# Product 4 in a second Strassen step, in 18 of the 20 projection groups

## The reference

```
h = rmsnorm(x); proj = h @ w_in                     # 1024 x 14336
b, c, xv, z, q, k, v, z_b, g_a, g_b = split(proj)
y_a = (b * (conv3(c * xv) + bias) * silu(z)) @ w_a_out
q, k = rotary(q), rotary(k) / 16                    # 4 heads of 256
o    = chunkwise retention(q, k, v), decay per head # v: 4 heads of 512
y_b  = (rmsnorm(o) * silu(z_b)) @ w_b_out
out  = rmsnorm(x + (sigmoid(g_a) * y_a + sigmoid(g_b) * y_b) @ w_o)
```

## Time and profile before

| | |
|---|---|
| median of 3 runs | 1380.13 us |
| profiled execution | 1379.97 us, of which the span of the trace 1378.2 us |
| PE busy | 1366.2 us (99%) |
| DVE busy | 995.4 us (72%) |
| ACT, POOL busy | 575.3 us (42%), 392.4 us (28%) |
| one conv group / one turn group | 38.08 / 38.46 us |

### The profile page before, as it was taken

How to read it: one execution, slowest core, us unless ns; L and a number is a source line. 1 busy time by engine, 2 the same in 40 slices (tenths; PEclk the granted TensorE clock), 3 DMA queues, 4 the chain that set the end, 5 groups by cost and what they waited for, 6 DMA issues and landing times.

```text
span 1378.2 us, 16016 instructions
## 1 busy us (share of the span) xinstructions
PE 1366.2 (99%) x6174; PEld 1130.5 (82%) x6174; DVE 995.4 (72%) x952; ACT 575.3 (42%) x779; POOL 392.4 (28%) x276
## 2 busy tenths in 40 slices
PE   9999999999999999999999999999999999999997
PEld 8788888888888888888888888888888888888886
DVE  6898434356556555678988888647777898778897
ACT  7843233222222222233333333337787433433445
POOL 0100222233334444443344444315545000100012
PEclk9999999999999999999999999999999999999999
DMA  9646313322221222355443444547767689945443
GB/s 335 182 161 209 112 57 107 123 77 77 77 63 61 67 71 61 92 153 153 142 119 111 134 138 140 195 170 244 273 223 267 140 314 329 240 162 198 156 89 122
DMA packets 105035, 211.64 MB, mean 154 GB/s; under 512 B 6912, under 2 KB 48000, under 8 KB 100096
## 3 DMA queue, kind: packets, MB, share of 16 engines
q1 hardware_dynamic: 101936, 192.77, 41.9%
q0 software_dynamic: 2880, 17.83, 6.6%
q10 hardware_dynamic: 144, 0.02, 0.0%
HBM read 147.68 MB, written 54.53 MB: 147 GB/s over the span
## 4 chain that ended last, share of the span: by engine, by line
PE 90%; DVE 3%; ACT 2%; issue 2%; DMA 1%; POOL 1%; SPq 1%; POOLq 0%; ACTq 0%; DVEq 0%
PE psum L2282 19%; PE psum L2284 18%; PE psum L2285 18%; PE psum L2416 7%; PE psum L2417 7%; PE psum L2418 7%; PE psum L2250 2%; PE psum L2253 2%; PE psum L2252 2%; PE psum L2327 2%; PE psum L2329 2%; PE psum L2328 2%; DMA raw_b<-x_t 1%; PE psum L2368 1%; DMA value_scratch<-value_c 1%
## 5 line engine op out<-in xcount | busy, mean ns | idle before, releaser
L2282 PE MATMUL psum<-hc,slots 128*128 128x512 f32 x1120 | 436.3, 390 | 0.9
L2285 PE MATMUL psum<-hc,slots 128*128 128x512 f32 x1120 | 435.8, 389 | 0.0
L2284 PE MATMUL psum<-hc,slots 128*128 128x512 f32 x1120 | 435.8, 389 | 0.0
L1004 ACT ACTIVATE slots<-work 128x1024 fp32r<-128x1024 f32 x140 | 148.7, 1062 | 510.2 <-PE psum L2285 414.9
L2282 PEld LDWEIGHTS psum<-hc,slots 128*128 128x128 f32 x1120 | 210.2, 188 | 47.2 <-issue 3.6
L1479 DVE TENSOR_TENSOR slots<-work,slots 128x1024 fp32r<-128x1024 f32 x140 | 185.5, 1325 | 86.8 <-ACT slots L1004 86.8
L2285 PEld LDWEIGHTS psum<-hc,slots 128*128 128x128 f32 x1120 | 210.2, 188 | 43.6
L2284 PEld LDWEIGHTS psum<-hc,slots 128*128 128x128 f32 x1120 | 210.2, 188 | 43.4
L1254 ACT ACTIVATE last_slot<-arena 128x1024 fp32r<-128x1024 f32 x112 | 118.6, 1062 | 163.2 <-PE psum L2418 155.7
L2416 PE MATMUL psum<-last_slot 128*128 128x512 f32 (+1 forms) x452 | 175.3, 388 | 0.0
L2417 PE MATMUL psum<-last_slot 128*128 128x512 f32 (+1 forms) x452 | 175.0, 387 | 0.0
(11 more groups left out here) (188 smaller groups left out, 1826.7 us busy)
## 6 DMA issues: line engine op xcount, KB each, us to landing
work<-w_channel SPq DMA_DIRECT2D x80, 512.0 KB, 3.6
arena<-w_last SPq DMA_DIRECT2D x19, 1024.0 KB, 7.5
qk<-qk_scratch SPq DMA_DIRECT2D x32, 512.0 KB, 3.4
arena<-w_last POOLq DMA_DIRECT2D x9, 1024.0 KB, 10.5
v_raw<-value_scratch SPq DMA_DIRECT2D x32, 256.0 KB, 3.9
arena<-gate_scratch SPq DMA_DIRECT2D x16, 512.0 KB, 6.9
value_c<-w_value SPq DMA_DIRECT2D x10, 512.0 KB, 4.2
rows_of_x<-x_rows SPq DMA_DIRECT2D x8, 512.0 KB, 9.3
```

The costliest lines, as they stand in the source:

```text
L1004: nc.scalar.activation(slots[:, u % SLOTS, 0, :], src, ACT.Copy).then_inc(w_hi, 1)
L2282: nc.tensor.matmul(bank, slot[:, 0, w], x_high, start=product in STARTS and j == 0, stop=False, skip_group_check=True)
L2284: nc.tensor.matmul(bank, slot[:, 0, w], x_low, start=False, stop=False, skip_group_check=True)
L2285: last = nc.tensor.matmul(bank, slot[:, 1, w], x_high, start=False, stop=j == 3, skip_group_check=True)
```

## The change

In groups 1 to 18 (`TWICE`) product 4 is itself done by a Strassen step on quarters: its d quadrant of weights is cut in four (columns of `work`, in the new `TILE_ORDER`), and so is T4 of h, in two halves of depth and two halves of 256 tokens. Seven products of quarters replace eight; each is 2 tiles of depth by 3 matmuls of 256 columns, so 42 matmuls of 256 columns stand for 24 of 512. Product 4 becomes two units. The first has the products of the plain weights of quarters 11, 12 and 21; the second has four products of sums of weights. POOL makes those sums in place after the low part of the first unit (`second_sums`, four operations of 128x256), and only then are they split, as 768 columns.

Three products go straight into the banks of product 4. The others go to two banks that the next group's product 6 is to use (`second_bank`), and DVE adds them to the group's sum: `second_first` after the first unit, `second_rest` (three operations) after the second. PE's last quarter product accumulates in the bank that `second_first` reads, so it waits for it. The next group's product 6 waits for `second_rest`. The sums of h's quarters are made once, in group 0, by DVE and ACT; the third goes over a part of T4, whose old content is kept in HBM and loaded again for group 19. `s1(g+1)` now waits for the low part of the second unit. The area for software DMA descriptors is set to 4 KB to make room.

```diff
+TWICE = range(1, GROUPS - 1)
+UNIT_TABLE = [(g, p) for g in range(GROUPS) for p in range(8 if g in TWICE else 7)]
+TILE_ORDER = [(0, 0), (0, 1), (0, 2), (0, 3), (1, 2), (1, 3), (1, 0), (1, 1)]
...
         def s1(g):
-            pool.wait_ge(w_ready, unit_at(g - 1, 4) + 1 if g else unit_of(1, 3, 1) + 1)
+            pool.wait_ge(w_ready, ended_at(g - 1) + 1 if g else unit_of(1, 3, 1) + 1)
...
+        def second_sums(g):
+            d = work[ROLES[g]["d"]]
+            a11, a12, a22, a21 = (d[:, n * QUARTER:(n + 1) * QUARTER] for n in range(4))
+            pool.wait_ge(w_ready, unit_at(g, 4) + 1)
+            nc.gpsimd.tensor_tensor(a22, a21, a22, ALU.add).then_inc(summed, 1)
+            nc.gpsimd.tensor_tensor(a21, a11, a21, ALU.subtract).then_inc(summed, 1)
+            pool.wait_ge(summed, second_summed(g, 1))
+            nc.gpsimd.tensor_tensor(a11, a22, a11, ALU.subtract).then_inc(summed, 1)
+            pool.wait_ge(summed, second_summed(g, 3))
+            nc.gpsimd.tensor_tensor(a12, a12, a11, ALU.subtract).then_inc(summed, 1)
...
+            if g in TWICE:
+                second_sums(g)
             if g + 1 < GROUPS:
                 s1(g + 1)
...
+        def second_first(g):
+            dve.wait_ge(unit_done, unit_at(g, 4) + 1)
+            at = tp_v[g % 2][:, 0, 0:QUARTER]
+            nc.vector.tensor_tensor(at, psum[:, second_bank(g), 0:QUARTER], at, ALU.add).then_inc(value_sum, 1)
+        def second_rest(g):
+            dve.wait_ge(unit_done, ended_at(g) + 1)
...
+                nc.vector.tensor_tensor(at, product, at, ALU.add).then_inc(value_sum, 1)
...
             if VALUE_UNITS < u <= UNITS:
-                g, n = divmod(u - 1 - VALUE_UNITS, 7)
-                if ORDER[n] not in (1, 2):
+                g, n = place_of(u - 1)
+                if n == 6 and g in TWICE:
+                    second_first(g)
+                elif n == 7:
+                    second_rest(g)
+                    add(g, 4)
+                elif ORDER[n] not in (1, 2):
                     add(g, ORDER[n])
             if u + 2 < UNITS:
                 low(u + 2)
...
+        def second_units(g):
+            u, x, z = unit_at(g, 4), set_at(g, 4), second_bank(g)
...
+            product_of_quarters(u, 0, quarter(0), one_six, start=True)
+            product_of_quarters(u, 1, quarter(2), c11)
+            product_of_quarters(u, 2, second("T4"), c21).then_inc(unit_done, 1)
+            pe.wait_ge(w_ready, u + 2)
+            product_of_quarters(u + 1, 2, second("T1"), five, start=True)
+            product_of_quarters(u + 1, 3, second("T3"), seven, start=True)
+            product_of_quarters(u + 1, 1, quarter(3), c12)
+            pe.wait_ge(value_sum, second_added(g, 1))
+            product_of_quarters(u + 1, 0, second("T2"), one_six).then_inc(unit_done, 1)
...
         def unit(g, product):
+            if product == 6 and g - 1 in TWICE:
+                pe.wait_ge(value_sum, second_added(g - 1, 4))
...
-    nc = bacc.Bacc("TRN2", target_bir_lowering=False, num_devices=1)
+    nc = bacc.Bacc("TRN2", target_bir_lowering=False, num_devices=1, dynamic_dma_scratch_size=4 * KB)
```

More of the change, by code:

```diff
@@ L95, in unit_at, with ended_at, columns_of, place_of @@
 def unit_at(g, product):
-    return VALUE_UNITS + 7 * g + ORDER.index(product)
+    return VALUE_UNITS + UNIT_TABLE.index((g, ORDER.index(product)))
+def ended_at(g):
+    return unit_at(g, 4) + (g in TWICE)
+def columns_of(u):
+    return 3 * QUARTER if u >= VALUE_UNITS and place_of(u)[0] in TWICE and place_of(u)[1] == 6 else 2 * HALF
+def place_of(u):
+    return UNIT_TABLE[u - VALUE_UNITS] if u < UNITS else (GROUPS, u - UNITS)
+def summed_until(g):
+    return 16 + 4 * g + 4 * len([n for n in TWICE if n < g])
+def second_summed(g, n):
+    return summed_until(g) + 4 + n
+def second_added(g, n):
+    return 20 + 4 * (g - TWICE.start) + n
 def before(order, product):
@@ L585, in _ @@
         stores = {"gate": gate_stores, "conv": conv_stores, "turn": turn_stores}
+        sp.wait_ge(h_ready, made(4))
+        for part in range(2):
+            sp.dma_start(kept_d[:, part], t4_part(1, part).bitcast(F32)).then_inc(x_in[4], 16)
         for g in range(GROUPS):
@@ L1365, in _ @@
                 continue
-            g, p = divmod(u - VALUE_UNITS, 7)
+            g, p = place_of(u)
+            if g == 0 and p == 5:
+                for name in ("T1", "T2", "T4"):
+                    second_high(name)
+            if g == TWICE.start and p == 2:
+                second_high("T3")
             if 0 < g <= GROUPS:
@@ L2254, in value_unit, with product_of_quarters, quarter, second @@
             last.then_inc(unit_done, 1)
+        def second_units(g):
+            u, x, z = unit_at(g, 4), set_at(g, 4), second_bank(g)
+            c11, c12, c21 = (psum[:, x + n // 2, n % 2 * QUARTER:(n % 2 + 1) * QUARTER] for n in range(3))
+            one_six, five, seven = psum[:, z, 0:QUARTER], psum[:, z + 1, 0:QUARTER], psum[:, z + 1, QUARTER:HALF]
+            def product_of_quarters(unit, place, right, to, start=False):
+                slot = slots[:, unit % SLOTS]
+                for j in range(2):
+                    w = slice((2 * place + j) * P, (2 * place + j + 1) * P)
+                    high, low = (right(part)[:, j, :] for part in range(2))
+                    nc.tensor.matmul(to, slot[:, 0, w], high, start=start and j == 0, stop=False, skip_group_check=True)
+                    nc.tensor.matmul(to, slot[:, 0, w], low, start=False, stop=False, skip_group_check=True)
+                    last = nc.tensor.matmul(to, slot[:, 1, w], high, start=False, stop=j == 1, skip_group_check=True)
+                return last
+            def quarter(n):
+                return lambda part: t4_part(n, part)
+            def second(name):
+                return lambda part: second_part(name, part)
+            pe.wait_ge(w_ready, u + 1)
+            pe.wait_ge(sum_made, 5 * g + sums_until(ORDER, 7))
+            if g == TWICE.start:
+                pe.wait_ge(h_ready, made(3) + 4)
+            product_of_quarters(u, 0, quarter(0), one_six, start=True)
[7 more added lines that the diff above has]
+            product_of_quarters(u + 1, 0, second("T2"), one_six).then_inc(unit_done, 1)
         def unit(g, product):
@@ L2394, in _ @@
                     retention_begins(product)
-                unit(g, product)
+                if product == 4 and g in TWICE:
+                    second_units(g)
+                else:
+                    unit(g, product)
         for s in range(1, STEPS):
```

101 lines of the change are left out of this document (84 added, 17 removed).

## The result

The changed kernel takes 1429.59 us (median of 4 runs, 1427.93 to 1430.65) against 1380.06 us: the ratio is 1.0355, 95% interval 1.0342 to 1.0368. It is 3.6% slower, where 1414 us (1402 to 1430) was predicted: 0.4 us inside the upper end of the range. The profiled execution took 1430.65 us, the longest of the four.

What follows compares the result with a forecast made beforehand. The prediction took PE to bound the kernel, busy 1366.2 of 1378.2 us. Its terms summed as 1379.97 - 7.5 + 38.7 - 1.2 + 0.8 + 3.5 = 1414.3 us, forecast 1414 us, range 1402 to 1430 (8 in 10).

Steps and rivals of the forecast that it cites:

- rival C: In the 8 turn groups: the forecast's stall plus the lower clock each time, about 2.5 us each, 1431 us; chance 0.13.
- PE as the bound, no stall hidden: Whole kernel: PE, busy 1366.2 of 1378.2 us, is the bound; every idle moment given to it is paid.
- DVE and POOL exclude each other: In turn groups: DVE operations with two SBUF inputs and POOL's never run together; 2.78 us against 0.68 us.
- The stall in the turn groups: In 8 turn groups: PE waits for `second_first` before product 4's last quarter product, 4.84 us each, 38.7 us in all.
- The clock: Behind the turn groups' stalls: the lower clock costs 1.3 us in one group in three, 3.5 us in all.
- The conv groups: In front of product 6 in 8 conv groups: PE waits 0.1 us each for `second_rest`, 0.8 us in all.
- The arithmetic: In product 4 of 18 groups: 256-column matmuls at 0.1196 us save 0.42 us a group, 7.5 us in all.
- Product 2's stall: In front of product 2, 8 times: the stall loses 0.15 us of its 0.38 us, -1.2 us in all.
- A: In turn groups: POOL leaves DVE alone, the stall is 0.74 us, 1378.0 us, not slower; chance 0.03.
- D: In product 4: the wait for `second_first` is met in time, leaving the arithmetic gain alone, 1373.3 us; chance 0.02.
- B: In turn groups: `s3` blocks the low part, turning steps slip past `s2`; stall 1.66 us, 1385.4 us; chance 0.06.
- Other edits: Extra operations in group 0, T4's store and reload, smaller descriptor area: 0 us, at most a few.

Runs made afterwards that it cites:

- filled run: Changed kernel plus five zero-weight float32 matmuls of 512 columns ahead of PE's wait for `second_first` in the turn groups; 1416.26 us, ratio 1.0269.
- POOL held back: Changed kernel, but in the turn groups POOL's `s2`, with the silu behind it, waits until `second_first` is done; 1429.10 us, ratio 1.0356.
- steps behind: Changed kernel with DVE's turning steps 0 to 2 moved directly behind `second_first` in the turn groups; 1416.23 us, ratio 1.0259.
- everything reordered: Changed kernel with `second_rest` right behind `second_first`, turning steps 0 to 2 in the next pass, ACT's product 1 copy ahead of its turned copies; 1410.78 us, ratio 1.0216.

## Why the prediction was right

The direction, the cause and the main term were right. The time itself is at the very end of the range, and that it is inside is in part luck: the forecast's own range ended at 1424, and the case that came is rival C, 1431 us, the lower clock each time. Against the 1414.3 us of the sum the profiled execution has 12.3 us more for the clock, 4.0 for the conv groups, 2.1 for its late start, 0.7 in group 19 and 0.2 for the stalls, and 1.7 and 1.5 us less for the arithmetic and for product 2.

- **PE as the bound, no stall hidden.** This was right: the terms under "Where the 50.4 us are" add up with nothing covered.
- **DVE and POOL exclude each other.** This was right in each duration: step 1 took 2.71 us and step 2 1.74 with POOL beside them, and 0.69 and 0.68 us when POOL was held back.
- **The stall in the turn groups.** 38.7 us were predicted and 38.9 measured. The predicted chain met its times within 0.2 us (low part 3.5 against 3.7, `s2` 6.3 against 6.5, step 2 8.6 against 8.7, PE 9.07 against 9.09), read in group 16. The gap is the same in groups 12 to 17; in groups 10 and 11 it is 0.5 us less and 0.6 us more. One thing in it was wrong, and it is wrong in the text on the change as well: I gave the 768 columns to the second unit. It is the first that has them; the second has 1024, so its low part comes later and product 4's earlier, and the two nearly cancel. The low parts of the two units in group 16:

```profile
834.86 0.95 DVE L1573 TENSOR_TENSOR slots<-work,slots 128x768 fp32r<-128x768 f32 x1
...
840.85 1.23 DVE L1573 TENSOR_TENSOR slots<-work,slots 128x1024 fp32r<-128x1024 f32 x1 [0.46 <-ACT slots L1082]
```

- **The clock, 3.5 us: the term mis-sized most.** The traces show 15.0 us, or 15.8 with the slower start behind each gap. I took one group in three at 1.3 us, and it was all eight at 1.9 us each. The 3.8 us without a fall were weighed as if they made it unlikely, though they are one case; in six of the eight stalls the granted clock was at 0.50 before PE started again. The filled run shows cause and size.
- **The conv groups, 0.8 us: 4.8.** The place and the wait were right (`second_rest` behind the low part of product 6, PE in front of product 6). `second_rest` ended 0.4 us later than worked out, at 10.7 instead of 10.33. About 0.3 us of this is the second unit's low part, 1.22 us for 1024 columns where the sum had 0.95 for 768, and all that follows moves with it. PE was ready at 10.37 where the sum had 10.46, and lost another 0.12 us behind the wait. With a margin of 0.1 us, an error of 0.4 in the chain is paid in full in each group.
- **The arithmetic, -7.5 us: -9.2.** A matmul of 256 columns takes 0.1174 us instead of the 0.1196 from the 24 of the earlier trace rows.
- **Product 2's stall, -1.2 us: -2.7.** Not 0.15 but all of the 0.38 us went, in the seven groups that had it. With the clock down in product 1, DVE and ACT had over a microsecond more; in the filled run, at full clock, a stall of that size is there. So this part of the gain was bought by the slow matmuls.
- **Rivals.** A and D did not come: the steps do meet POOL, and the wait is not met in time. B did not come: POOL takes the first free moment. C, the lower clock each time, is what happened, at 1.9 us a group instead of the 2.5 us it was given. Its chance of 0.13 was too small, and its 1431 us is close to the measured time in part because the conv groups, for which it had 0.8 us too, and the late start, which it did not have, make up for what it had too much.
- **Other edits.** They cost nothing, as predicted: the run without the turn groups has them all and takes the time of the kernel before.

## What to carry to other kernels

A cheaper way to multiply that gives PE a new wait in the middle must be read from the list of the engine that it waits for. Here three operations ahead of one read cost 38.9 us of stalls and 15.0 us of slow matmuls, against a gain of 9.2 us; moving the three gave back 13 us, and putting the lists in another order some 50. Where two engines exclude each other, as DVE and POOL here, an operation released by the end of the one before it can meet the next one. Take blocked durations, not bare ones, and see where the displaced work waits next. Start with the part of the program whose helpers have slack (here the conv groups), and price every PE gap of some microseconds with the slower matmuls behind it: about 2 us in this kernel.

## What the runs showed of the hardware

- The lower clock came with all eight stalls of the changed kernel, gaps of 4.4 to 5.6 us from start to start, and cost 1.9 us each. It came too with the gaps in front of product 6 of 3.3 to 3.6 us (POOL held back) and of 2.95 to 3.6 us (steps behind), with seven of 3.2 to 3.3 us in front of product 5 (everything reordered), and with one of 2.26 us in the products for v (changed kernel). It did not come with the gap of 3.14 us in front of product 5 of group 11 (everything reordered), nor with those of 1.3 to 2.5 us in product 4 (POOL held back). So from 2.3 to 3.1 us both were seen, and the length of the gap alone does not decide.
- At 1.2 GHz matmuls of 512 columns follow each other after 0.427 us, of 256 columns after 0.214 us, against 0.2267 and 0.1174 us at 2.4 GHz (changed kernel).
- Float32 matmuls with zero weights held the clock: five of 512 columns, ten entries in the trace, 4.45 us in each stall, and it stayed at 1.00.
- POOL's operations of 128x256 take 0.74 us each with no DVE operation of two SBUF inputs beside them (the estimate from the two wider ones was 0.75), and 1.11 to 1.19 us for the first two in a turn group, where DVE's L1835 and L1837 are beside them.
